# The Mamba-2 scan of one diffusion trunk step on one core: masks made by TensorE, ln dt in the exponents, outputs three steps behind

## Chip, cores and metric

One NeuronCore of a Trainium2 chip runs the whole kernel as one launch. The metric is the device time of a launch in microseconds (us); smaller is better.

## The reference, cut to what matters

The kernel computes four layers of a diffusion backbone for 128 context tokens and 256 latent tokens. Layer 1 mixes its tokens with a bidirectional Mamba-2 scan (SSD), and the change touches that layer alone. For each direction the scan is, in chunks of 128 tokens:

```python
acs = jnp.cumsum(dtc * a.reshape(SSD_GROUPS, r), axis=2)
seg = acs[:, :, :, None] - acs[:, :, None, :]
decay = jnp.exp(jnp.where(lower, seg, -jnp.inf))
cb = jnp.einsum('bcign,bcjgn->bcijg', cc, bc)
wts = cb[..., None] * decay * dtc[:, :, None]
y_diag = jnp.einsum('bcijgr,bcjgrp->bcigrp', wts, xc)
to_end = jnp.exp(acs[:, :, -1:] - acs) * dtc
chunk_states = jnp.einsum('bcjgn,bcjgr,bcjgrp->bcgrpn', bc, to_end, xc)
y_off = jnp.einsum('bcign,bcgrpn->bcigrp', cc, h_prev) * jnp.exp(acs)[..., None]
```

There are 32 heads of 64 in 8 groups of 4 heads, a state of 128, and two directions (forward f, backward b), whose outputs are added. The result is multiplied by silu(z), normalised and multiplied by `ssd_w_out`.

## The kernel before, in words

The program is written by hand, engine by engine, and counting semaphores order the work. Matrices of the layers are float32 split into a high and a low float32r part: ScalarE (ACT) rounds each chunk of weights of 128 x 1024 (`round_to`, L829), and POOL and VectorE (DVE) subtract one half each (`low_to`, L700 and L1183). TensorE (PE) makes three products per tile. Four chunks are held at once.

The SSD layer has these stages. `ssd_conv` makes x, B and C. `dt_prepare` makes 16 z tiles (PE, about 4.25 us each), and beside them dt, the running sums of dt times a (`neg_cum`, `back_cum`), and at its end the tables `to_end` and `full_decay` (ACT L959, L960, DVE L1381). The scan then runs 24 steps: for each of 8 groups g, chunk c = 0 (the context), 1 and 2 (the two latent halves); u = 3g + c counts steps and v counts latent steps. In each step u the engines do, in program order:

- PE (`scan_pe`): three transposes and C times B into bank u % 2 (L1854 to L1857); the chunk state of step u - 1 (L1842, two products when c = 0, else one); for each direction four products that spread the running sum of one head over a 128 x 128 square (L1866, stationary adt, moving the triangle tri, float32) into bank 2 + d; and the output of step u - 2 (L1833). An output has per head two terms of `x_dt` times `decay`, and for a latent chunk two more of a state times `c_scaled`: 16 products of 64 stationary columns in a latent step, 8 in a context step.
- ACT (`scan_act`): copies bank u % 2 to SBUF (L969); for latent chunks two exponentials of 512 columns (L975) for `c_scaled`; four Relu of 128 columns for the backward exponents (L981); two exponentials of 512 columns (L990).
- DVE (`scan_dve`): `take_state(u - 1)` (L1407, or L1415 and L1420); two triangular masks of C times B (L1430); four forward exponents of 128 columns (L1439); after each exponential a product with the masked C times B (L1449); the output of step u - 2 into xbc (L1394).
- POOL (`scan_pool`): `x_end` (L740, two when c = 0), `x_dt` of both directions (L748), and for latent chunks two products of `c_scaled` with C (L756).
- SP (`scan_traffic`) loads a group's start state and stores its context state, 256 KB each; its queue also carries all weight loads.

`ssd_end` then runs over 16 tiles m of y: DVE multiplies by silu(z) (L1469) and makes `y_lo` of tile m - 1 (L1464); ACT squares (L998) and rounds (`y_hi`, L999); POOL adds the squares (L766, L769). In each m every engine also prepares weight chunk m + 2 of `ssd_out`:

```python
for m in range(KI):
    low_to(n0 + min(m + 3, KI))
    pool.wait_ge(y_sq_ready, m + 1)
```

PE makes `ssd_out` beside this (L1727 to L1729, 18 products of 512 columns per chunk, 288 in all), waits for each `y_lo` and weight chunk, and before chunk 12 for the sum of squares (L1892).

Of the kernel before, what the change touches and what calls it, by code (L numbers as in the profile page):

```python
# [14 lines left out]
P = 128  # L15
# [27 lines left out]
SCAN_LAG = 2  # L43
SCAN_SLOTS = SCAN_LAG + 1
DT_DVE = 20
# [33 lines left out]
SLOTS = 4  # L79
# [67 lines left out]
def build_trunk(nc, a, out):  # L147
# [4 lines left out]
    with ExitStack() as ctx:  # L152
# [7 lines left out]
        h_hi = sb("h_hi", [P, KD, COLS], F32R)  # L160
        h_lo = sb("h_lo", [P, KD, COLS], F32R)
# [7 lines left out]
        rowc = sb("rowc", [P, D])  # L169
        junk = sb("junk", [P, D], BF16)  # L170
# [47 lines left out]
        with ExitStack() as part:  # L218
            zt = sb("zt", [P, KI, COLS], F32, part)
            xbc = sb("xbc", [P, CONV_TILES, COLS], F32, part)  # L220
            state0 = sb("state0", [P, 2, 2, GW], F32, part)
            dtv = sb("dtv", [P, 3, NDT], F32, part)
            adt = sb("adt", [P, 3, NDT], F32, part)
            neg_cum = sb("neg_cum", [P, 3, NDT], F32, part)
            back_cum = sb("back_cum", [P, 3, SSD_HEADS], F32, part)
# [42 lines left out]
        decay = [by_dir(flat_mod[:, k * 1024:(k + 1) * 1024]) for k in range(SCAN_SLOTS)]  # L268
        c_scaled = [by_dir(flat_mod[:, 3072:4096]), by_dir(flat_gb[:, 1024:2048])]
        turned = flat_gb[:, 0:1024].rearrange("p (u n) -> p u n", u=2)  # L270
        x_dt = [by_dir(flat_wk[:, k * 512:(k + 1) * 512]) for k in range(SCAN_SLOTS)]
# [4 lines left out]
        state1 = by_dir(flat_stage[:, 896:1408])  # L276
        cb_mask = by_dir(flat_stage[:, 1408:1664])
# [82 lines left out]
        s_seg_back = sem("s_seg_back")  # L360
        s_exp = sem("s_exp")
        s_w = sem("s_w")
        s_xdt = sem("s_xdt")
# [107 lines left out]
        def z_bank(m):  # L471
            return bank((2, 3, 7)[m % 3])

# [218 lines left out]
        def _(pool):  # L692
# [39 lines left out]
            def scan_pool():  # L732
                for g, c, u, v in steps():
                    pool.wait_ge(s_copied, u + 1)
                    xt = turned[:, u % 2, P:P + GW].rearrange("p (h q) -> p h q", h=HPG)
# [8 lines left out]
                    if u >= SCAN_SLOTS:  # L744
                        pool.wait_ge(s_y, u - SCAN_SLOTS + 1)
                    for d in range(2):
                        h0 = d * SSD_HEADS + g * HPG
                        pool.tensor_tensor(x_dt[u % SCAN_SLOTS][:, d, :].rearrange("p (h q) -> p h q", h=HPG), xt,  # L748
                                           dtv[:, c, h0:h0 + HPG].unsqueeze(2).broadcast_to([P, HPG, HEAD]),
                                           ALU.mult).then_inc(s_xdt, 1)  # L750
                    if c:
                        for d in range(2):
                            pool.wait_ge(s_cexp, 2 * v + d + 1)
                            cs = c_scaled[v % 2][:, d, :].rearrange("p (h i) -> p h i", h=HPG)
# [64 lines left out]
        def _(act):  # L819
# [128 lines left out]
            def dt_prepare():  # L948
# [9 lines left out]
                act.wait_ge(z_dt, DT_DVE - 1)  # L958
                act.activation(to_end, to_end, ACT.Exp).then_inc(dt_act, 1)  # L959
                act.activation(full_decay, full_decay, ACT.Exp).then_inc(dt_act, 1)  # L960

            def scan_act():
                for g, c, u, v in steps():
                    act.wait_ge(s_turned, u + 1)
                    if u >= 2:
                        act.wait_ge(s_state, u - 1)
                        act.wait_ge(s_xdt, 2 * (u - 1))
                        act.wait_ge(s_w, 2 * (u - 2) + 2)
                    act.activation(turned[:, u % 2, :], bank(u % 2), ACT.Copy).then_inc(s_copied, 1)  # L969
                    if c:  # L970
                        if v >= 2:
                            act.wait_ge(s_y, latent_step(v - 2) + 1)
                        for d in range(2):
                            act.wait_ge(s_cum, 2 * u + d + 1)
                            act.activation(c_scaled[v % 2][:, d, :], bank(2 + d), ACT.Exp).then_inc(s_cexp, 1)  # L975
                    if u >= SCAN_SLOTS:
                        act.wait_ge(s_y, u - SCAN_SLOTS + 1)
                    act.wait_ge(s_cum, 2 * u + 2)
                    for h in range(HPG):
                        hs = slice(h * P, (h + 1) * P)  # L980
                        ins = act.activation(decay[u % SCAN_SLOTS][:, 1, hs], bank(3)[:, hs], ACT.Relu, scale=-1.0,  # L981
                                             bias=back_cum[:, c, g * HPG + h:g * HPG + h + 1])
                    ins.then_inc(s_seg_back, 1)
                    for d in range(2):
                        if d:
                            act.wait_ge(s_seg_back, u + 1)
                        else:
                            act.wait_ge(s_seg, u + 1)
                        w = decay[u % SCAN_SLOTS][:, d, :]
                        act.activation(w, w, ACT.Exp, scale=-1.0 if d else 1.0).then_inc(s_exp, 1)  # L990

            def ssd_end():
                n0 = lin["ssd_out"].n0
                for m in range(KI):
# [6 lines left out]
                    round_to(n0 + min(m + 3, KI))  # L1001
# [169 lines left out]
        def _(vec):  # L1171
# [168 lines left out]
            def dt_prepare():  # L1340
# [26 lines left out]
                link(vec.scalar_tensor_tensor(out=adt[:, :, :], in0=rowc[:, 960:1024].unsqueeze(1).broadcast_to([P, 3, NDT]),  # L1367
                                              scalar=-1.0, in1=dtv[:, :, :], op0=ALU.mult, op1=ALU.mult))
                assert n[0] == DT_DVE - 2
# [867 lines left out]
```

## Time and profile before

| what | value |
|---|---|
| time, median of 3 runs | 2129.44 us (2127.71 to 2131.0) |
| time of the profiled execution | 2127.83 us |
| its span | 2126.1 us |
| PE busy | 1967.0 us, 93% |
| DVE / ACT / POOL busy | 58% / 44% / 35% |
| granted PE clock, mean | 0.965 |
| the scan, first to last PE or DVE instruction | 637.3 to 783.4 us |
| `ssd_out` on PE | 785.9 to 875.9 us |

The span is what the trace covers; the time has 1.7 us more around it. An engine's busy time counts its own instructions alone. Times in the views are in us from the start of the span; "xN" is a count of records, and a float32 product of PE leaves two records, a float32r product one. The length of a PE record holds its way through the array; the distance between the starts of two records is what the stream pays.

### The profile page before, as it was taken

The numbers are of one execution on the slowest core, as the hardware profiler recorded it, in microseconds if no ns is written. First come the engines' busy times: TensorE is split into PE (matmuls) and PEld (weight loads), VectorE is DVE, ScalarE is ACT, GpSimd is POOL, SyncE is SP. The second block draws the span as 40 slices with busy tenths as digits, with TensorE's granted clock in tenths as the row PEclk, the third lists the DMA queues.
The fourth block names the chain that finished last, engine by engine and source line by source line (L and its number), as shares of the span: only waits on it lengthen the run. The fifth ranks groups of instructions, "written<-read, shape, count | busy, mean of one in ns | idle before, by whom it ended". The sixth has DMA issues, their size and how long they took to land.

```text
span 2126.1 us, 30500 instructions
## 1 busy us (share of the span) xinstructions
PE 1967.0 (93%) x11921; PEld 1752.3 (82%) x11921; DVE 1237.2 (58%) x1888; ACT 926.9 (44%) x1522; POOL 736.8 (35%) x563
## 2 busy tenths in 40 slices
PE   3779999999998878899999998899999979899998
PEld 1569998799997876699988875699987857799986
DVE  0567771466617867677742873777733675677732
ACT  1244442444536644454432534544433434544422
POOL 0033334332346646232333651233233321233242
PEclk6889999999999999999999999999999979999999
DMA  9963437544330123743455564543454512244432
GB/s 367 385 234 122 128 101 247 178 129 123 107 113 26 31 114 120 280 147 120 128 184 192 201 193 157 222 148 120 129 201 159 207 55 100 80 141 127 121 127 79
DMA packets 80671, 326.44 MB, mean 154 GB/s; under 512 B 9073, under 2 KB 17809, under 8 KB 66705
## 3 DMA queue, kind: packets, MB, share of 16 engines
q1 hardware_dynamic: 78928, 322.57, 43.7%
q8 instruction: 95, 1.56, 0.3%
q10 hardware_dynamic: 1600, 1.93, 0.3%
q14 instruction: 48, 0.39, 0.1%
HBM read 319.34 MB, written 5.12 MB: 153 GB/s over the span
## 4 chain that ended last, share of the span: by engine, by line
PE 78%; DVE 7%; ACT 5%; DMA 4%; issue 4%; POOL 3%; SPq 1%; DVEq 0%; ACTq 0%; POOLq 0%
PE pair L1693 17%; PE pair L1695 17%; PE pair L1694 17%; PE pair L1728 6%; PE pair L1727 6%; PE pair L1729 6%; PE pair L1833 2%; DVE x L1250 1%; DMA mod_more<-in_w_mod 1%; PE pair L1915 1%; POOL w_lo L700 1%; PE pair L1866 1%; DMA raw<-in_pool 1%; ACT junk L857 1%; DMA ssd_cols<-in_ssd_cols 1%
## 5 line engine op out<-in xcount | busy, mean ns | idle before, releaser
L700 POOL TENSOR_TENSOR w_lo<-raw,w_hi 128x512 fp32r<-128x512 f32 (+1 forms) x375 | 575.5, 1536 | 1165.3 <-ACT w_hi L829 1165.3
L1693 PE MATMUL pair<-h_hi,w_hi 128*128 128x386 f32 (+1 forms) x2008 | 689.0, 343 | 18.3 <-POOL h_lo L707 15.7
L1695 PE MATMUL pair<-h_hi,w_lo 128*128 128x386 f32 (+1 forms) x2008 | 684.6, 341 | 0.0
L1694 PE MATMUL pair<-h_lo,w_hi 128*128 128x386 f32 (+1 forms) x2008 | 683.9, 341 | 0.0
L1183 DVE TENSOR_TENSOR w_lo<-raw,w_hi 128x512 fp32r<-128x512 f32 x351 | 427.4, 1220 | 331.7 <-ACT w_hi L829 331.6
L829 ACT ACTIVATE w_hi<-raw 128x1024 fp32r<-128x1024 f32 x375 | 393.1, 1050 | 285.9 <-PE pair L1729 222.7
L1693 PEld LDWEIGHTS pair<-h_hi,w_hi 128*128 128x128 f32 (+1 forms) x2008 | 381.7, 190 | 23.7 <-POOL h_lo L707 21.6
L1694 PEld LDWEIGHTS pair<-h_lo,w_hi 128*128 128x128 f32 (+1 forms) x2008 | 382.3, 190 | 0.9
L1695 PEld LDWEIGHTS pair<-h_hi,w_lo 128*128 128x128 f32 (+1 forms) x2008 | 381.6, 190 | 0.3
L1307 DVE SCALAR_TENSOR_TENSOR acc<-pair,taps,acc 128x385 f32<-128x385 f32 x176 | 109.0, 619 | 214.1 <-ACT acc L916 214.1
L916 ACT ACTIVATE acc<-pair,taps 128x386 f32<-128x386 f32 x176 | 117.2, 666 | 237.9 <-PE pair L1695 237.9
L1728 PE MATMUL pair<-w_hi,g 128*128 128x512 f32 x528 | 208.6, 395 | 0.0
L1729 PE MATMUL pair<-w_lo,g 128*128 128x512 f32 x528 | 208.6, 395 | 0.0
L1727 PE MATMUL pair<-w_hi,g 128*128 128x512 f32 x528 | 208.5, 395 | 0.0
L1728 PEld LDWEIGHTS pair<-w_hi,g 128*128 128x128 f32 x528 | 99.4, 188 | 23.2
L1727 PEld LDWEIGHTS pair<-w_hi,g 128*128 128x128 f32 x528 | 99.3, 188 | 23.3
L1729 PEld LDWEIGHTS pair<-w_lo,g 128*128 128x128 f32 x528 | 99.3, 188 | 23.2
L914 ACT ACTIVATE g<-gate 128x386 fp32r<-128x386 f32 x84 | 44.3, 528 | 162.4 <-DVE gate L1320 162.4
L1314 DVE SCALAR_TENSOR_TENSOR acc<-pair,taps,acc 128x385 f32<-128x385 f32 x176 | 108.6, 617 | 3.2
L707 POOL TENSOR_TENSOR h_lo<-stage,h_hi 128x512 fp32r<-128x512 f32 x21 | 32.0, 1522 | 88.9 <-ACT h_hi L879 88.9
L1833 PE MATMUL pair<-mod_raw,wk 128*64 128x128 f32 x384 | 45.4, 293 | 16.2 <-DVE stage L1420 9.7
L1664 PE MATMUL pair<-mod_raw,cond 128*32 128x256 f32 x512 | 36.4, 425 | 23.3 <-DMA mod_raw<-in_w_mod 23.3
(251 smaller groups left out, 2302.2 us busy)
## 6 DMA issues: line engine op xcount, KB each, us to landing
raw<-in_ffn_in SPq DMA_DIRECT2D x176, 512.0 KB, 3.5
raw<-in_ffn_out SPq DMA_DIRECT2D x88, 512.0 KB, 3.5
mod_raw<-in_w_mod SPq DMA_DIRECT2D x32, 1024.0 KB, 7.7
mod_base<-in_w_mod SPq DMA_DIRECT2D x31, 1024.0 KB, 7.4
mod_more<-in_w_mod SPq DMA_DIRECT2D x20, 1024.0 KB, 13.0
raw<-in_ssd_conv SPq DMA_DIRECT2D x32, 512.0 KB, 3.5
gb<-rows_dram SPq DMA_DIRECT2D x8, 1024.0 KB, 5.0
raw<-in_ssd_z SPq DMA_DIRECT2D x16, 512.0 KB, 3.5
```

The source lines that it names most:

```text
L700: pool.tensor_tensor(w_lo[:, m % SLOTS, 0:w], raw[:, m % SLOTS, 0:w], w_hi[:, m % SLOTS, 0:w].bitcast(F32), ALU.subtract).then_inc(w_low_p ...
L829: act.activation(w_hi[:, m % SLOTS, 0:w], raw[:, m % SLOTS, 0:w], ACT.Copy).then_inc(w_rounded, 1)
L916: act.activation(acc[:, j % 4, :], tile_bank(j)[:, 0:COLS], ACT.Identity, scale=taps[:, l, j, 1:2], bias=taps[:, l, j, 3:4]).then_inc(acc_ ...
L1183: vec.tensor_tensor(w_lo[:, m % SLOTS, w0:w1], raw[:, m % SLOTS, w0:w1], w_hi[:, m % SLOTS, w0:w1].bitcast(F32), ALU.subtract).then_inc(w_ ...
L1307: vec.scalar_tensor_tensor(out=acc[:, j % 4, 1:COLS], in0=b[:, 0:COLS - 1], scalar=taps[:, l, j, 0:1], in1=acc[:, j % 4, 1:COLS], op0=ALU. ...
L1314: vec.scalar_tensor_tensor(out=acc[:, j % 4, 0:COLS - 1], in0=b[:, 1:COLS], scalar=taps[:, l, j, 2:3], in1=acc[:, j % 4, 0:COLS - 1], op0= ...
L1693: ten.matmul(to, wh, h_hi[:, k, cols], start=k == 0, stop=False, skip_group_check=True)
L1694: ten.matmul(to, wh, h_lo[:, k, cols], start=False, stop=False, skip_group_check=True)
L1695: ins = ten.matmul(to, wl, h_hi[:, k, cols], start=False, stop=k == KD - 1, skip_group_check=True)
L1727: ten.matmul(to, hi[:, k, cols], wh, start=first, stop=False)
L1728: ten.matmul(to, lo[:, k, cols], wh, start=False, stop=False)
L1729: ins = ten.matmul(to, hi[:, k, cols], wl, start=False, stop=last)
```

## The change

- The running sums are made once as rows (`cum_rows`, a float32r high part and a low part in other partitions; 12 float32 products into bank 4 in `dt_prepare`), and PE spreads a head's row with the 0/1 column of `head_row` (float32r, 128 columns moving). A further float32r product of 512 moving columns (`outside_of`) adds -2^100 outside the triangle, after ACT has read the bank for `c_scaled` where c > 0.
- The exponents get `shift` = ln dt minus the running sum as ACT's bias, so x needs no product with dt, and ACT writes both directions with 8 exponentials of 128 columns (`one_way`). DVE adds the two directions and multiplies the sum once with C times B, which it reads from PSUM. A head's output has one term for both directions in place of two.
- DVE in place of ACT copies bank u % 2 (384 columns of it), at the head of its step.
- The exponents go round banks 2, 3 and 7; PE waits for `s_exp` (ACT). Outputs are three steps behind and come in two halves between the `outside_of` products. `turned` and `decay` have 4 slots, `c_scaled` 3, `state1` 2.
- Ln of dt, the exponentials of `to_end` and `full_decay` and the copy of `cum_rows` are in ACT's order after z tiles 3 and 6.
- `ssd_end` prepares a weight chunk at m = 8, 10, 12 and 14 and the rest after the loop.

The diff, cut (leading blanks taken off):

```diff
-SCAN_LAG = 2
+SCAN_LAG = 3
 SCAN_SLOTS = SCAN_LAG + 1
-DT_DVE = 20
+C_SLOTS = 3
+DT_ADT = 18
+DT_DVE = DT_ADT + 3
+FAR = 2.0 ** 100
+DT_LEAST = 1e-37
...
-neg_cum = sb("neg_cum", [P, 3, NDT], F32, part)
-back_cum = sb("back_cum", [P, 3, SSD_HEADS], F32, part)
+shift = sb("shift", [P, 3, NDT], F32, part)
+ident_r = sb("ident_r", [P, P], F32R, part)
+outside = sb("outside", [P, 2, P], F32R, part)
...
+decay = [flat_mod[:, k * 512:(k + 1) * 512] for k in range(SCAN_SLOTS)]
+one_way = [[flat_mod[:, 2048 + d * 1024 + k * 512:2560 + d * 1024 + k * 512] for d in range(2)] for k in range(2)]
...
+state1 = [[under_h_lo[:, 2 * k + d, AT[1]:AT[1] + GW] for d in range(2)] for k in range(2)]
...
+def seg_bank(u, d):
+
+return bank((2, 3, 7)[(2 * u + d) % 3])
...
-        if u >= SCAN_SLOTS:
-            pool.wait_ge(s_y, u - SCAN_SLOTS + 1)
-        for d in range(2):
-            h0 = d * SSD_HEADS + g * HPG
-            pool.tensor_tensor(x_dt[u % SCAN_SLOTS][:, d, :].rearrange("p (h q) -> p h q", h=HPG), xt,
-                               dtv[:, c, h0:h0 + HPG].unsqueeze(2).broadcast_to([P, HPG, HEAD]),
-                               ALU.mult).then_inc(s_xdt, 1)
...
-        low_to(n0 + min(m + 3, KI))
+        low_to(n0 + SLOTS + max(0, m - 6) // 2)
...
+    low_to(n0 + KI)
...
         z_evac(m)
-    act.wait_ge(z_dt, DT_DVE - 1)
-    act.activation(to_end, to_end, ACT.Exp).then_inc(dt_act, 1)
-    act.activation(full_decay, full_decay, ACT.Exp).then_inc(dt_act, 1)
+        if m == 3:
+            act.wait_ge(z_dt, DT_ADT + 1)
+            act.activation(log_dt, log_dt, ACT.Ln).then_inc(dt_act, 1)
+        if m == 6:
+            act.wait_ge(z_dt, DT_DVE - 1)
+            act.activation(to_end, to_end, ACT.Exp).then_inc(dt_act, 1)
+            act.activation(full_decay, full_decay, ACT.Exp).then_inc(dt_act, 1)
+            act.wait_ge(dt_pe, 3)
+            act.activation(cum_rows[:, :, :], bank(4)[:, 0:3 * P].rearrange("p (c i) -> p c i", c=3),
+                           ACT.Copy).then_inc(dt_act, 1)
...
     for g, c, u, v in steps():
-        act.wait_ge(s_turned, u + 1)
...
-        act.activation(turned[:, u % 2, :], bank(u % 2), ACT.Copy).then_inc(s_copied, 1)
...
-        act.wait_ge(s_cum, 2 * u + 2)
...
-            ins = act.activation(decay[u % SCAN_SLOTS][:, 1, hs], bank(3)[:, hs], ACT.Relu, scale=-1.0,
-                                 bias=back_cum[:, c, g * HPG + h:g * HPG + h + 1])
-        ins.then_inc(s_seg_back, 1)
+                act.activation(c_scaled[v % C_SLOTS][:, d, :], seg_bank(u, d), ACT.Exp).then_inc(s_cexp, 1)
         for d in range(2):
-            if d:
-                act.wait_ge(s_seg_back, u + 1)
-            else:
-                act.wait_ge(s_seg, u + 1)
-            w = decay[u % SCAN_SLOTS][:, d, :]
-            act.activation(w, w, ACT.Exp, scale=-1.0 if d else 1.0).then_inc(s_exp, 1)
+            act.wait_ge(s_seg, 2 * u + d + 1)
+            if u >= 2:
+                act.wait_ge(s_sum, u - 1)
+            to = one_way[u % 2][d]
+            for h in range(HPG):
+                hs = slice(h * P, (h + 1) * P)
+                col = d * SSD_HEADS + g * HPG + h
+                ins = act.activation(to[:, hs], seg_bank(u, d)[:, hs], ACT.Exp, bias=shift[:, c, col:col + 1])
+            ins.then_inc(s_exp, 1)
...
+    link(vec.tensor_scalar(log_dt, flat_dt, DT_LEAST, None, ALU.max))
...
+    ch.did(vec.tensor_tensor(head_row[:, :].rearrange("p (d h) -> p d h", d=2), halves[:, :, 0, :],
...
+    ch.did(vec.tensor_copy(ident_r[:, :], ident[:, :]))
+    ch.did(vec.tensor_scalar(outside[:, :, :], tri[:, :, :], 1.0, FAR, ALU.subtract, ALU.mult))
...
-    ch.did(vec.tensor_scalar(neg_cum[:, :, :], cum, -1.0, None, ALU.mult))
+    vec.wait_ge(dt_act, 3)
     ch.did(vec.tensor_copy(full_decay, total))
-    ch.did(vec.tensor_copy(back_cum[:, :, :], cum[:, :, SSD_HEADS:]))
+    ch.did(vec.scalar_tensor_tensor(out=shift[:, :, :], in0=cum, scalar=-1.0,
+                                    in1=log_dt.rearrange("p (c h) -> p c h", c=3), op0=ALU.mult, op1=ALU.add))
     ch.wait()
-    link(vec.tensor_tensor(to_end, full_decay, neg_cum[:, :, :], ALU.add))
+    link(vec.tensor_tensor(to_end, full_decay, cum, ALU.subtract))
+    low_to(lin["ssd_z"].n0 + 10)
+    vec.wait_ge(dt_act, 6)
+    link(vec.tensor_tensor(to_end, to_end, dtv[:, :, :], ALU.mult))
+    for d in range(2):
+        low_rows = slice((2 * d + 1) * SSD_HEADS, (2 * d + 2) * SSD_HEADS)
+        vec.tensor_tensor(cum_rows[low_rows, :, :], bank(4)[low_rows, 0:3 * P].rearrange("p (c i) -> p c i", c=3),
+                          cum_rows[low_rows, :, :].bitcast(F32), ALU.subtract).then_inc(s_rows, 1)
     low_to(lin["ssd_out"].n0 + SLOTS)
-    vec.wait_ge(dt_act, 4)
-    link(vec.tensor_tensor(to_end, to_end, dtv[:, :, :], ALU.mult))
...
-        if g:
-            vec.wait_ge(s_y, 3 * g)
+        if g >= 2:
...
+        vec.wait_ge(s_turned, u + 1)
...
+        vec.tensor_copy(turned[u % SCAN_SLOTS][:, 0:P + GW], bank(u % 2)[:, 0:P + GW]).then_inc(s_copied, 1)
...
-        vec.wait_ge(s_copied, u + 1)
-        if u:
-            vec.wait_ge(s_w, 2 * u)
-        for d in range(2):
-            ch.did(vec.tensor_tensor(cb_mask[:, d, :], turned[:, u % 2, P + GW:], tri[:, d, :], ALU.mult))
-        masks = ch.n
-        if u >= SCAN_SLOTS:
-            vec.wait_ge(s_y, u - SCAN_SLOTS + 1)
...
-        for h in range(HPG):
-            col = g * HPG + h
-            ins = vec.tensor_scalar(decay[u % SCAN_SLOTS][:, 0, h * P:(h + 1) * P], bank(2)[:, h * P:(h + 1) * P],
-                                    neg_cum[:, c, col:col + 1], 0.0, ALU.add, ALU.min)
...
-        for d in range(2):
-            vec.wait_ge(s_exp, 2 * u + d + 1)
-            w = decay[u % SCAN_SLOTS][:, d, :].rearrange("p (h i) -> p h i", h=HPG)
-            vec.tensor_tensor(w, w, cb_mask[:, d, :].unsqueeze(1).broadcast_to([P, HPG, P]),
-                              ALU.mult).then_inc(s_w, 1)
+        vec.wait_ge(s_exp, 2 * u + 2)
+        to = decay[u % SCAN_SLOTS]
+        vec.tensor_tensor(to, one_way[u % 2][0], one_way[u % 2][1], ALU.add).then_inc(s_sum, 1)
+        vec.wait_ge(s_sum, u + 1)
+        w = to.rearrange("p (h i) -> p h i", h=HPG)
+        vec.tensor_tensor(w, w, bank(u % 2)[:, P + GW:].unsqueeze(1).broadcast_to([P, HPG, P]),
+                          ALU.mult).then_inc(s_w, 1)
         if u >= SCAN_LAG:
             output(*ALL_STEPS[u - SCAN_LAG][:3])
...
+    for c in range(3):
+        for d in range(2):
+            hs = slice(d * SSD_HEADS, (d + 1) * SSD_HEADS)
+            for rows in range(2 * d, 2 * d + 2):
+                ins = ten.matmul(bank(4)[rows * SSD_HEADS:(rows + 1) * SSD_HEADS, c * P:(c + 1) * P],
+                                 adt[:, c, hs], tri[:, d, :], start=True, stop=True, skip_group_check=True)
+    ins.then_inc(dt_pe, 1)
...
+    def output(g, c, u, v, heads):
+        if heads[0] == 0:
...
+            ten.wait_ge(s_w, u + 1)
...
+        for h in heads:
...
-            terms = [(x_dt[u % SCAN_SLOTS][:, d, hs], decay[u % SCAN_SLOTS][:, d, ws]) for d in range(2)]
+            terms = [(turned[u % SCAN_SLOTS][:, P + h * HEAD:P + (h + 1) * HEAD], decay[u % SCAN_SLOTS][:, ws])]
             if c:
...
+        if heads[-1] == HPG - 1:
+            ins.then_inc(s_y, 1)
+
+    def outside_of(u, d):
+        ten.matmul(seg_bank(u, d), ident_r[:, :], outside[:, d, :].unsqueeze(1).broadcast_to([P, HPG, P]),
+                   start=False, stop=True, skip_group_check=True).then_inc(s_seg, 1)
...
+            ten.wait_ge(s_w, u - 1)
...
         if u:
             states((u - 1) % 3, u - 1)
         for d in range(2):
-            if u:
-                ten.wait_ge((s_seg, s_seg_back)[d], u)
+            i = 2 * u + d - 3
+            if i >= 0:
+                ten.wait_ge(s_exp, i + 1)
             for h in range(HPG):
                 col = d * SSD_HEADS + g * HPG + h
-                ins = ten.matmul(bank(2 + d)[:, h * P:(h + 1) * P],
-                                 adt[:, c, col:col + 1].broadcast_to([P, P]), tri[:, d, :],
-                                 start=True, stop=True, skip_group_check=True)
+                ins = ten.matmul(seg_bank(u, d)[:, h * P:(h + 1) * P], head_row[:, col:col + 1].broadcast_to([P, P]),
+                                 cum_rows[:, c, :], start=h == 0, stop=False, skip_group_check=True)
             ins.then_inc(s_cum, 1)
-        if u >= SCAN_LAG:
-            output(*ALL_STEPS[u - SCAN_LAG])
+            if not c:
+                outside_of(u, d)
+        for d in range(2):
+            if u >= SCAN_LAG:
+                output(*ALL_STEPS[u - SCAN_LAG], range(2 * d, 2 * d + 2))
+            if c:
+                ten.wait_ge(s_cexp, 2 * v + d + 1)
+                outside_of(u, d)
     states(2, 3 * GROUPS - 1)
     for step in ALL_STEPS[-SCAN_LAG:]:
-        output(*step)
+        output(*step, range(HPG))
```

## Rows read from the trace of the kernel before

**Rows 1.** By stretch of the scan: PE, PEld, DVE, ACT, POOL busy; clock; DMA.

```profile
637.28:650.49 13.21, 11.64 (x85) 10.68 (x86) 8.55 (x20) 8.45 (x21) 7.97 (x11) 0.87 0.06 20
650.49:775.75 125.26, 108.10 (x1061) 99.55 (x1060) 103.22 (x258) 76.04 (x180) 84.30 (x102) 0.99 0.09 29
775.75:783.42 7.67, 7.02 (x64) 6.78 (x64) 1.21 (x4) 0.00 (x0) 0.00 (x0) 0.65 0.01 2
```

**Rows 2.** Chain of waits in the scan: start us, us, what.

```profile
707.88 2.54 PE pair L1833 x32
...
723.88 0.43 DVE stage L1420
...
742.03 2.54 PE pair L1833 x32
```

**Rows 3.** Timeline of steps: start us, us, engine, line [idle before, releaser].

```profile
699.77 1.95 PE L1866 MATMUL pair<-tri,adt 128*128 128x128 f32 x16
...
700.92 0.60 ACT L975 ACTIVATE gb<-pair 128x512 f32<-128x512 f32 x1 [0.79 <-PE pair L1866]
...
702.25 1.14 ACT L981 ACTIVATE mod_raw<-pair,back_cum 128x128 f32<-128x128 f32 x4
...
702.72 0.33 PE L1854 MATMUL pair<-ident,xbc 128*128 128x128 f32 x1
...
703.33 0.60 PE L1842 MATMUL pair<-wk,gb 128*128 128x256 f32 x2
...
709.52 1.15 ACT L990 ACTIVATE mod_raw<-mod_raw 128x512 f32<-128x512 f32 x2 [2.57 <-DVE mod_raw L1439]
...
710.25 1.29 DVE L1449 TENSOR_TENSOR mod_raw<-mod_raw,stage 128x512 f32<-128x512 f32 x2 [0.77 <-ACT mod_raw L990]
...
711.46 0.60 DVE L1394 SCALAR_TENSOR_TENSOR xbc<-xbc,ssd_cols,pair 128x128 f32<-128x128 f32 x2
...
712.02 0.69 DVE L1407 COPY stage<-pair 128x512 f32<-128x512 f32 x1
...
739.31 1.64 POOL L740 TENSOR_TENSOR wk<-gb,stage 128x256 f32<-128x256 f32 x2 [0.41 <-ACT gb L969]
```

**Rows 4.** Timeline of the last z tile's end and of the scan's first instruction.

```profile
633.38 0.49 ACT L945 ACTIVATE zt<-pair 128x386 f32<-128x386 f32 x1 [2.81 <-PE pair L1695]
...
637.28 0.30 PE L1854 MATMUL pair<-ident,xbc 128*128 128x128 f32 x1 [3.94 <-DVE stage L1381]
```

**Rows 5.** Timeline of float32r products in a row, of 512 and 256 moving columns.

```profile
811.49 0.40 PE L1728 MATMUL pair<-w_hi,y_lo 128*128 128x512 f32 x1
...
811.72 0.40 PE L1729 MATMUL pair<-w_lo,y_hi 128*128 128x512 f32 x1
...
1723.44 0.28 PE L1996 MATMUL pair<-w_hi,h_lo 128*128 128x256 f32 x1
1723.56 0.28 PE L1997 MATMUL pair<-w_lo,h_hi 128*128 128x256 f32 x1
```

**Rows 6.** DVE lines of the scan: ns min/median/max, first and last start.

```profile
L1449 DVE TENSOR_TENSOR mod_raw<-mod_raw,stage x48: 677/692/1124, 643.2 to 773.5; 128x512 f32<-128x512 f32 x48
...
L1420 DVE TENSOR_TENSOR stage<-stage,pair x16: 420/421/423, 650.3 to 775.1; 128x256 f32<-128x256 f32 x16
```

**Rows 7.** Timeline of ssd_out, its two long waits.

```profile
799.18 0.77 PE L1727 MATMUL pair<-w_hi,y_hi 128*128 128x512 f32 x1 [4.73 <-DVE y_lo L1464]
...
855.38 0.77 PE L1892 MATMUL pair<-ones,stage 128*128 128x1 f32 x3 [7.61 <-POOL stage L769]
```

**Rows 8.** Lines of ssd_end and ssd_out: ns min/median/max, first and last start.

```profile
L1469 DVE TENSOR_TENSOR xbc<-xbc,zt x16: 553/1647/1657, 783.4 to 852.4; 128x386 f32<-128x386 f32 x16
...
L1729 PE MATMUL pair<-w_lo,y_hi x96: 386/394/629, 786.5 to 875.5; 128*128 128x512 f32 x96
```

**Rows 9.** Groups by line, 783 to 856 us: busy, mean ns, idle before.

```profile
L700 POOL TENSOR_TENSOR w_lo<-raw,w_hi 128x512 fp32r<-128x512 f32 x12 | 21.5, 1792 | 29.0 <-ACT w_hi L829 29.0
...
L829 ACT ACTIVATE w_hi<-raw 128x1024 fp32r<-128x1024 f32 x12 | 12.6, 1050 | 12.8 <-DMA raw<-in_ssd_out 7.2 <-PE pair L1729 5.6
```

More of the change, by code:

```diff
@@ L160, in build_trunk @@
         h_hi = sb("h_hi", [P, KD, COLS], F32R)
+        with ExitStack() as part:
+            under_h_lo = sb("under_h_lo", [P, KD, COLS], F32, part)
         h_lo = sb("h_lo", [P, KD, COLS], F32R)
@@ L169, in build_trunk @@
         rowc = sb("rowc", [P, D])
+        with ExitStack() as part:
+            cum_rows = sb("cum_rows", [P, 3, P], F32R, part)
+            head_row = sb("head_row", [P, NDT], F32R, part)
         junk = sb("junk", [P, D], BF16)
@@ L266, in by_dir @@
             return ap.rearrange("p (d n) -> p d n", d=2)
[L268 to L271, printed above, removed]
+        decay = [flat_mod[:, k * 512:(k + 1) * 512] for k in range(SCAN_SLOTS)]
+        one_way = [[flat_mod[:, 2048 + d * 1024 + k * 512:2560 + d * 1024 + k * 512] for d in range(2)] for k in range(2)]
+        c_scaled = [by_dir(flat_gb[:, 1024:2048]), by_dir(flat_wk[:, 512:1536]), by_dir(rowc[:, :])]
+        turned = [flat_gb[:, 0:512], flat_gb[:, 512:1024], flat_wk[:, 0:512], flat_stage[:, 1408:1920]]
+        adt = flat_wk[:, 512:704].rearrange("p (c h) -> p c h", c=3)
+        log_dt = flat_wk[:, 704:896]
         x_end = by_dir(flat_wk[:, 1536:2048])
@@ L1432, in scan_dve @@
-                    if u >= SCAN_SLOTS:
-                        vec.wait_ge(s_y, u - SCAN_SLOTS + 1)
-                    vec.wait_ge(s_cum, 2 * u + 1)
-                    if c:
-                        vec.wait_ge(s_cexp, 2 * v + 1)
-                    for h in range(HPG):
-                        col = g * HPG + h
-                        ins = vec.tensor_scalar(decay[u % SCAN_SLOTS][:, 0, h * P:(h + 1) * P], bank(2)[:, h * P:(h + 1) * P],
-                                                neg_cum[:, c, col:col + 1], 0.0, ALU.add, ALU.min)
-                        if h == HPG - 1:
-                            ins.then_inc(s_seg, 1)
-                        else:
-                            ch.did(ins)
@@ L1828, in output @@
                         if c:
                             for d in range(2):
-                                st = state0[:, g % 2, d, hs] if d == c - 1 else state1[:, d, hs]
-                                terms.append((st, c_scaled[v % 2][:, d, ws]))
+                                st = state0[:, g % 2, d, hs] if d == c - 1 else state1[g % 2][d][:, hs]
+                                terms.append((st, c_scaled[v % C_SLOTS][:, d, ws]))
                         for n, (lhs, rhs) in enumerate(terms):
@@ L1841, in states @@
                     for d in state_dirs(c):
-                        ins = ten.matmul(bank(6)[:, d * GW:(d + 1) * GW], turned[:, u % 2, 0:P], x_end[:, d, :],
+                        ins = ten.matmul(bank(6)[:, d * GW:(d + 1) * GW], turned[u % SCAN_SLOTS][:, 0:P], x_end[:, d, :],
                                          start=True, stop=True, skip_group_check=True)
@@ L1898, in free @@
                     ten.wait_ge(s_taken, 3 * GROUPS)
-                    ten.wait_ge(s_exp, 6 * GROUPS)
+                    ten.wait_ge(s_w, 3 * GROUPS)
                 out_product(sums, 2, y_hi, y_lo, ready, free)
```

66 lines of the change are left out of this document (29 added, 37 removed).

## The prediction, made before the changed kernel was built

> **What bounds the kernel now.** I read the busy times by stretch first. The scan lasts 146.1 us [rows 1]: 13.2 for three steps without an output, 125.3 in the middle, 7.7 at the end. In the middle PE is busy 86% and DVE 82%, so neither engine alone sets the pace. The chain of waits says what does: it repeats every 34.15 us for six steps (742.03 - 707.88), 17.08 us per group [rows 2], and goes from PE's outputs through ACT's Relu and exponentials to DVE's products and `take_state` and back to PE. In each step DVE works before the exponentials (masks, forward exponents) and after them, and PE waits for its last piece. The second stretch is `ssd_out`: 18 products a chunk at 0.23 us [rows 5] are 4.19 us, 67 us in all, but it lasts from 785.9 to 875.9 [rows 8], 90 us. PE waits 4.7 us for a `y_lo` and 7.6 us for the sum of squares [rows 7], some 0.7 us at each of four more tiles, and after each long wait runs slower: the products there take 0.77 us, not 0.40 [rows 5, 7]. The cause is that each tile of y stands in line behind a weight chunk on three engines.
>
> **The scan, engine by engine.** Prices per product of PE are distances of starts: transposes with C times B 0.61, a state product 0.44, four spread products 0.89, which is 0.222 each (1.95 us record groups less the last record's length, 16 records at 0.111) [rows 3]. A latent output of 16 products takes 2.54 us [rows 2].
>
> The spread products turn from float32 to float32r with 128 moving columns, which no row shows. From below: 256 columns cost 0.12 and 512 cost 0.23 [rows 5], a line that gives 0.062 at 128. From above: the old price, 0.222; nothing but that row caps it. I take 0.11, the distance of two weight loads of 128 columns within a float32 product, since such a load is now needed every 128 columns. The Trainium skill's page "TensorE: Matmul & The Clock Gate", section on LDWEIGHTS, makes a load of 128 columns 107 ns; by it the sum stays as it is, by the line of the moving columns alone it falls by 6 us.
>
> PE after, per step: eight spread products 0.89; two masks of 512 columns 0.46 [rows 5]; a latent output of 12 products, 12/16 of 2.54, 1.9, plus 0.2 for two more changes between 64 and 128 stationary columns (estimate), so outputs with masks 2.6; a context output 0.64. A context step is 0.61 + 0.44 + 0.89 + 0.46 + 0.64 = 3.04, the first latent 0.61 + 0.88 + 0.89 + 2.6 = 4.98, the second 4.54: 12.6 us per group. ACT: eight exponentials of 128 columns, 2.3 a step, as four Relu cost 1.14 [rows 3], plus 1.2 in latent steps: 9.3. DVE: copy 0.55 (384 of the 512 columns that cost 0.69), add and multiply 1.3, output 0.6, state 0.8: 9.8 a group, where it was 14.1 (82% of 17.08). POOL loses its two `x_dt` products per step. All three would fit beside PE.
>
> **The chain after.** What is late next is DVE's queue. The copy of step u + 1 stands behind the add and multiply of step u, which wait for ACT's last exponential, and that for PE's second mask. From PE's second mask of a second latent step: to ACT 0.26 (eight records from 699.77, ACT at 700.92), exponentials 1.14, to DVE 0.1, add and multiply 1.3, output 0.56, copy 0.55, to POOL 0.1, two `x_end` 1.64, to PE 0.2 [rows 3]: 5.85. DVE's add reads two operands from SBUF. The old product that does so takes 0.68 to 1.12 us, while a line with one operand in PSUM never leaves 0.42 [rows 6]; the long ones lie beside POOL's. POOL then holds a `c_scaled` product, 1.1 long, so I add 0.9 (bounds 0 and 1.2): 6.75. The Trainium skill's page "SBUF — State Buffer", section "SBUF: two separate sides", says that such an op and a GpSimd op exclude each other for a whole instruction. By this rule, which speaks against the new add, the period stays at my figure; without it it is 0.9 shorter. The rows agree.
>
> PE can take the context state only then, though its own work reaches that point after 3.65. Then: state 0.88, spread 0.89, output with masks 2.6 = 4.37, and the next latent step 4.54, whose states come in time. The group takes 6.75 + 4.37 + 4.54 = 15.7, against 17.1. The other new waits are covered: transposes wait for `s_w` of two steps before (2.8 after the mask, with the hop at 3.05, when PE is ready for them), the third bank's `s_exp` lies over 1 us back, the masks' wait for `s_cexp` lies beside half an output. SP's load of a start state waits for an output that comes one step later, but is used three steps on, some 15 us; the store of a context state has as long.
>
> Whole scan: three steps to fill, 13.2 scaled by 15.7/17.1, 12.1; seven groups 109.9. The end: DVE reaches the last `take_state` 4.3 after the last mask, 0.8 more, 0.25 to PE; the last two outputs, 32 products in 7.0 us at clock 0.65 [rows 1], are 24 now, 5.3 (0.65 is a mean of the clock's two levels, 1.2 and 2.4 GHz, after PE's wait, and I leave it so); DVE 0.8: 11.4. Sum 133.4, so **-12.7**.
>
> **Start.** PE sat 3.94 us at the scan's start for DVE L1381, after ACT's table and exponentials [rows 4]. These move under the z tiles, where ACT is idle 2.81 us per tile [rows 4] and its four table loads and the new waits on DVE and PE fit in; DVE's and POOL's next weight halves come about 1 us later but lie four chunks ahead, and SP's loads are freed by them with the same lead. If that cover failed it would cost up to 3 us. PE then starts after the last z evacuation, 633.9, so 3.3 earlier. The 12 new products are on PE's path: between 0.7 (four column groups side by side) and 2.7 (12 x 0.222), I take 1.0. **-2.3**.
>
> **ssd_out.** Without a chunk a tile costs DVE 0.55 and 0.6 (its minimum [rows 8]) and POOL 0.9, and these exclude each other: 2.0. Tile 8 comes at 799.5; its product, squares and rounding 1.7, round 1.05, low half 1.8 [rows 9]: chunk 4 is there at 804.0, PE wants it at 785.9 + 4 x 4.19 = 802.7: wait 1.3. From there two tiles and one chunk take 2.0 + 0.55 + 1.1 + 1.05 + 1.8 = 6.5 against 4.19: 2.3 for each of three chunks; then 0.3. Waits 8.5, products 67, unit transposes and sums 1.6: 77, not 90. In the rows no slow products follow the waits of 0.7 us; for waits of 2 us no row speaks, I count nothing and leave 3 us in the bounds. I take **-12.5** (bounds: -17 if nothing waits, -5 if tiles take 2.7 or the clock falls). `y_lo` and the sum are early, so 5 MB of loads for the next stage also start early; I count nothing for it.
>
> **Sum.** -12.7 - 2.3 - 12.5 = -27.5. The profiled execution is 2127.8 (span 2126.1 + 1.7), so 2100.3; the median is 1.6 above it, so **2102**.
>
> **Rivals.**
> - *Narrow float32r at the full old price* (0.222). For: no row below 256 columns. Against: 256 and 512 lie on a line. 16 products of the latent steps gain 0.11 less, 1.8 per group, 14 us in all: 2116. Chance 0.15.
> - *The DVE queue does not bind*, since copies come earlier than I think: PE's 12.6 per group, 3.1 x 7.8 = 24 less: 2078. For: DVE is 60% busy. Chance 0.25.
> - *The weights only change places*: tiles stay slow, PE waits for chunks 4 to 7 instead of `y_lo`, gain 5: 2110. This is the case where the change does not do what it says. Chance 0.10.
> - *Slower*: a float32r product with 128 moving columns that costs more than the float32 one it replaces. It stands in PE's order before the masks, on the chain above, 16 times a group, about 125 times. It decides from 0.11 + 27.5/125 = 0.33 us; at 0.40 the time is 2138. Against: the rows' line. Chance 0.04.
> - The rest, 0.46, is my forecast, of which 0.02 for gains lost to causes I don't see.
>
> **Numbers.** The range 2074 to 2118 reaches from below the PE-bound case (with the 0.062 price 2072 is possible) to above the dear float32r, and leaves out the slower case and the far ends. About 0.2% is what a measurement here tells from no change. Faster by more than that 0.94, within it 0.02, slower 0.04.
>
> **What would show it.** Scan near 133 us; a group near 15.7; spread products 0.11 apart; PE waiting for POOL's `x_end` before the context state, and nowhere else for long; PE's first scan instruction at most 0.6 after the last z evacuation; `ssd_out` near 77 us with waits for weights at chunks 4 to 7 and none for the sum of squares. The forecast is wrong if the spread products stand 0.2 apart, if PE waits for DVE's output or `take_state` in each step, or if z tiles grow beyond 4.25 us.

## The result, and the profile after the change

The changed kernel takes **2118.31 us** (median of 5 runs, 2116.47 to 2122.18); the kernel before, in 5 runs, 2129.93 (2127.71 to 2131.0). The ratio is 0.9949, 95% interval 0.9935 to 0.9964: 11.6 us faster, where 27.5 were forecast, and 0.3 us outside the range given. The profiled execution took 2119.51 us (span 2117.8); its mean granted clock is 0.954, where it was 0.965.

The busy times by stretch of the new scan, in the columns of [rows 1]: up to the first output, the middle, from the last state on. As outputs now lag by three steps, the first stretch holds four steps, where it held three.

```profile
636.90:654.20 17.30, 15.08 (x68) 12.55 (x68) 9.88 (x17) 11.62 (x33) 8.88 (x10) 0.70 0.04 16
654.20:778.95 124.75, 111.03 (x748) 91.15 (x748) 63.86 (x134) 61.36 (x191) 51.40 (x55) 0.82 0.09 29
778.95:790.50 11.55, 7.02 (x59) 6.08 (x58) 5.07 (x13) 1.14 (x4) 2.20 (x2) 0.70 0.00 0
```

Against [rows 1], DVE is busy 51% of the middle, not 82%, and PE 89%, although it has fewer products. The column of the clock says why: 0.82, where it was 0.99. The scan lasts 153.6 us, not 146.1 and not the forecast 133.4. One group in the timeline (start, length, engine, line; idle time before and releaser in brackets):

```profile
705.26 1.39 DVE L1449 TENSOR_TENSOR mod_raw<-mod_raw 128x512 f32<-128x512 f32 x1 [1.65 <-ACT mod_raw L993]
...
707.81 0.55 DVE L1444 COPY gb<-pair 128x384 f32<-128x384 f32 x1
...
708.44 1.78 POOL L754 TENSOR_TENSOR wk<-gb,stage 128x256 f32<-128x256 f32 x2 [2.33 <-DVE gb L1444]
...
710.32 1.10 PE L1859 MATMUL pair<-wk,gb 128*128 128x256 f32 x4 [2.06 <-POOL wk L754]
...
711.07 1.77 PE L1885 MATMUL pair<-cum_rows,head_row 128*128 128x128 f32 x8
...
714.73 0.80 PE L1850 MATMUL pair<-outside,ident_r 128*128 128x512 f32 x1
...
718.00 0.42 PE L1872 MATMUL pair<-ident,xbc 128*128 128x128 f32 x1
```

The forecast chain is there: add (L1449), copy behind it, POOL's `x_end`, then PE's context state, 6.5 us after the last mask of the second latent step (started at 703.55, its 512 columns 0.23 us, so about 703.8). But PE has stood idle for 2.06 us, and the latent step that follows takes 7.7 us, 710.32 to 718.00: its mask is a record of 0.80 us, where one of the step before took 0.50. The granted clock by stretch of the same group: the context step, the wait, the first latent step, the second.

```profile
704.00:707.50 3.50, 2.98 (x26) 2.40 (x25) 2.20 (x3) 2.90 (x11) 2.11 (x2) 1.00 0.47 150
707.50:710.30 2.80, 0.74 (x5) 0.58 (x6) 2.73 (x7) 0.42 (x2) 1.78 (x2) 1.00 0.00 0
710.30:718.00 7.70, 7.68 (x38) 6.21 (x39) 1.84 (x5) 2.34 (x6) 2.76 (x3) 0.58 0.02 4
718.00:722.80 4.80, 4.80 (x42) 4.08 (x41) 3.12 (x7) 3.33 (x10) 0.90 (x2) 0.97 0.00 0
```

A granted clock of 0.58 over the step means that most of it runs at the lower of the clock's two levels, 1.2 GHz; in the next step, at 0.97, 2.4 GHz is back. The waits of PE from the end of the z tiles to the end of `ssd_out` (in total, times, longest):

```profile
PE pair L1859 <- POOL wk L754: 14.5, 7, 2.2
PE pair L1845 <- DVE under_h_lo L1437: 3.8, 1, 3.8
PE pair L1731 <- POOL w_lo L714: 3.4, 2, 2.3
PE pair L1731 <- DVE y_lo L1467: 3.2, 1, 3.2
```

The start of the scan, against [rows 4], and `ssd_out`, against [rows 7, 8]:

```profile
636.35 0.49 ACT L953 ACTIVATE zt<-pair 128x386 f32<-128x386 f32 x1 [2.81 <-PE pair L1699]
...
636.90 0.33 PE L1872 MATMUL pair<-ident,xbc 128*128 128x128 f32 x1 [0.58 <-ACT zt L953]
...
821.03 0.50 PE L1731 MATMUL pair<-w_hi,y_hi 128*128 128x512 f32 x1 [1.15 <-POOL w_lo L714]
...
827.77 0.80 PE L1731 MATMUL pair<-w_hi,y_hi 128*128 128x512 f32 x1 [2.29 <-POOL w_lo L714]
...
850.32 0.72 PE L1916 MATMUL pair<-ones,stage 128*128 128x1 f32 x6
```

```profile
L1472 DVE TENSOR_TENSOR xbc<-xbc,zt x16: 545/1228/1654, 790.5 to 826.5; 128x386 f32<-128x386 f32 x16
...
L1733 PE MATMUL pair<-w_lo,y_hi x96: 387/394/632, 793.6 to 868.4; 128*128 128x512 f32 x96
```

PE has been idle for 0.58 us when it begins, and nearly all of that is the last z evacuation itself: it ends at 636.84, and PE begins at 636.90. The tiles of y come in 36 us, not 69; the sum of squares keeps nobody waiting; two waits for weights are left. The span's 8.3 us, by stretch (each z evacuation taken by its start): before the z evacuations +2.0 (nothing in the change touches that part; over the profiled executions of all kernels here the last z evacuation starts anywhere from 633.4 to 640.1), z tiles 65.1 to 66.1, +1.0; to PE's first scan instruction 3.9 to 0.55, -3.35; the scan +7.5; from there to the end of `ssd_out` 92.5 to 78.3, -14.2; the rest -1.2.

### The profile page after: what moved, and what is told of

The parts are those of the page before. It is cut to its first block, busy times and chain, and to the rows that moved or that the text cites. A ratio compares the mean times of both kernels' runs of the same rounds, so it can differ in the third digit from the quotient of the medians.

```text
span 2117.8 us, 29692 instructions
## 1 busy us (share of the span) xinstructions
PE 1975.0 (93%) x11609; PEld 1745.0 (82%) x11609; DVE 1199.7 (57%) x1773; ACT 920.3 (43%) x1552; POOL 703.9 (33%) x515
## 4 chain that ended last, share of the span: by engine, by line
PE 81%; DVE 6%; ACT 4%; DMA 3%; issue 3%; POOL 2%; SPq 1%; DVEq 0%; ACTq 0%; POOLq 0%
PE pair L1697 17%; PE pair L1699 17%; PE pair L1698 17%; PE pair L1731 6%; PE pair L1732 6%; PE pair L1733 6%; PE pair L1845 2%; DVE x L1255 2%; DMA mod_more<-in_w_mod 1%; PE pair L1939 1%; ACT junk L865 1%; DMA raw<-in_pool 1%; PE pair L1885 1%; PE pair L1850 1%; DVE wk L1246 1%
## 5 line engine op out<-in xcount | busy, mean ns | idle before, releaser
L993 ACT ACTIVATE mod_raw<-pair,shift 128x128 f32<-128x128 f32 x192 | 53.8, 375 | 33.4 <-PE pair L1850 33.2
```

## The experiments

Three questions: does the wait cost its length, or also the clock behind it; what makes the wait; and are the other two parts worth what was forecast? Each measured time stands against a median of the kernel before from the same chip; kernels compared with the same median ran on one chip. An idle product is one whose result nothing reads.

### The other two parts alone

`e4_end_only` is the kernel before with only the new places of the weight halves:

```diff
-                    low_to(n0 + min(m + 3, KI))
+                    low_to(n0 + SLOTS + max(0, m - 6) // 2)
...
+                low_to(n0 + KI)
```

(on DVE and POOL, and the same with `round_to` on ACT).

> The kernel before with only the last part of the change, the place of the weight chunks' halves among the tiles of y in ssd_out. Theory: this part alone gives 12 to 14 us whatever the scan does: ssd_out from 90 us to 76 to 78, kernel 2116 to 2118, so that the new scan and the new start are together worth nothing. Rival (it gains only because the changed scan leaves other conditions, banks and DVE free earlier): less than 6 us, 2124 or more.

Measured 2117.29 us against 2130.48, ratio 0.9938 (0.9924 to 0.9951): -13.2. The part does not need the new scan.

`e8_start_only` is the kernel before with only this (and, on DVE, the product behind it, with the weight halves placed round it as in the changed kernel):

```diff
                 for m in range(1, KI):
                     z_evac(m)
-                act.wait_ge(z_dt, DT_DVE - 1)
-                act.activation(to_end, to_end, ACT.Exp).then_inc(dt_act, 1)
-                act.activation(full_decay, full_decay, ACT.Exp).then_inc(dt_act, 1)
+                    if m == 6:
+                        act.wait_ge(z_dt, DT_DVE - 1)
+                        act.activation(to_end, to_end, ACT.Exp).then_inc(dt_act, 1)
+                        act.activation(full_decay, full_decay, ACT.Exp).then_inc(dt_act, 1)
```

> The kernel before with only ACT's table and exponentials for the decays (and DVE's product behind them) moved under the z tiles; no new rows, no new products. Theory: PE starts the scan 0.6 us after the last z evacuation instead of 3.9, so 3.3 us are gained if nothing later takes them back: 2127 us. Rival (the first steps of the scan wait for DVE anyway): no change, 2130.

Measured 2126.68 against 2130.27, ratio 0.9982 (0.9973 to 0.9991): -3.6. With the 1.0 us of the small products these two parts make -15.8, more than the whole change's 11.6. So the new scan did not pay: it takes 7.5 us longer in the profiled execution. In the medians it costs some 4 us, a sum of three differences whose 95% intervals (about 3, 3 and 2 us to either side) together leave it uncertain by nearly 5, if the parts add up at all.

### The wait filled, and nothing else

`e5_fill` adds to the changed kernel, on PE:

```diff
+                def fillers(b, n):
+                    for _ in range(n):
+                        ten.matmul(b[:, 0:2 * P], ident_r[:, :], cum_rows[:, 0:2, :], start=True, stop=True,
+                                   skip_group_check=True)
...
+                    if c == 1:
+                        if u > 1:
+                            ten.wait_ge(s_exp, 2 * u - 2)
+                        fillers(seg_bank(u, 0), 16)
                     if u:
                         states((u - 1) % 3, u - 1)
```

> The changed kernel, its order untouched, with 16 idle float32r products of 256 columns (about 1.9 us by 0.12 each) on PE in the one long wait of each group, between the transposes and the context state, into a bank that ACT has done with. Nothing of the computation changes. Theory (the clock): that wait of 2.06 us lets the clock fall, and the first latent step then takes 7.7 us instead of 4.4; filled, the step is back at 4.4, the group at about 15.7 instead of 19.0, the kernel at 2118 - 7 x 3.3 = 2095 us, granted clock in the scan near 1. Rival A (the products of that step are slow in themselves): nothing moves, 2118. Rival B (DVE and POOL set the period, the clock costs nothing on the path): the step shrinks but the waits grow by as much, 2118.

Measured 2101.73 against 2130.12, ratio 0.9863 (0.9847 to 0.988): 16.6 us below the changed kernel, for work that computes nothing. A group of it in the timeline:

```profile
702.47 2.15 PE L1851 MATMUL pair<-cum_rows,ident_r 128*128 128x256 f32 x16
704.77 1.10 PE L1864 MATMUL pair<-wk,gb 128*128 128x256 f32 x4 [0.15 <-issue]
705.52 1.19 PE L1894 MATMUL pair<-cum_rows,head_row 128*128 128x128 f32 x8
...
709.57 0.27 PE L1877 MATMUL pair<-ident,xbc 128*128 128x128 f32 x1
```

The state comes as long after the mask as in the changed kernel (6.5 us), but the step behind it takes 4.8 us, not 7.7. Rivals A and B both fall: the same products are fast, and the time comes off the period. With the clock held, the scan, 639.4 to 773.2, takes **133.8 us**; the forecast was 133.4. `e10_fill_four` has 4 such products instead of 16.

> The changed kernel with 4 idle products (0.5 us) in each group's wait, not 16, so that 1.6 us of it stay. If a wait of 1.6 us is as bad as one of 2.06: 2118, groups of 19.0 us with half speed after the wait. If the shorter wait leaves the clock alone: 2101, as with 16. I lean to something between, since in e7_wait_back one and the same wait of 2.33 us let the clock fall in some groups and not in others: 2110.

Measured 2105.21 against 2130.27, ratio 0.9876 (0.9858 to 0.9893), with one execution at 2097.6. Waits of 1.58 us are left. From context state to context state the profiled execution takes 15.7 to 16.1 us three times, 17.1 and 17.6, and 19.2 once. In this execution the shorter wait brought the slow stretch less often.

### What makes the wait

`e2_copy_first` moves one instruction of DVE in the changed kernel: step u + 1's copy goes ahead of the add and multiply of step u.

```diff
+                copy(0)
                 for g, c, u, v in steps():
-                    vec.wait_ge(s_turned, u + 1)
-                    if u >= SCAN_SLOTS:
-                        vec.wait_ge(s_y, u - SCAN_SLOTS + 1)
-                    vec.tensor_copy(turned[u % SCAN_SLOTS][:, 0:P + GW], bank(u % 2)[:, 0:P + GW]).then_inc(s_copied, 1)
                     if u:
                         take_state(*ALL_STEPS[u - 1][:3])
+                    if u + 1 < 3 * GROUPS:
+                        copy(u + 1)
                     vec.wait_ge(s_exp, 2 * u + 2)
```

(`copy(u)` is the four lines taken out.)

> The changed kernel with DVE's copy of step u + 1 ahead of the add and multiply of step u. Theory (the copy behind the add and multiply is what delays POOL's x_end and so the context state): POOL is free of c_scaled some 2.3 us after the second mask, x_end 1.7, so the state can start about 4.2 us after the mask instead of 6.5; PE then waits only some 0.6 us for the multiply before its transposes. With the clock at full the group is 3.6 + 0.6 + 4.4 + 4.5 = 13.2 us, the kernel 2118 - 8 x 5.8 = 2072. If the clock falls all the same, only the 2.1 us of the wait go: 2101. Rival (POOL, not DVE's order, is late): 2112 to 2118.

`e3_act_copy` leaves DVE's order and gives the copy back to ACT, ahead of the step's exponentials:

```diff
+                    act.wait_ge(s_turned, u + 1)
+                    if u >= SCAN_SLOTS:
+                        act.wait_ge(s_y, u - SCAN_SLOTS + 1)
+                    act.activation(turned[u % SCAN_SLOTS][:, 0:P + GW], bank(u % 2)[:, 0:P + GW], ACT.Copy).then_inc(s_copied, 1)
                     if c:
```

> The changed kernel with the copy of the turned operands back on ACT, ahead of its exponentials of the step, as before the change. Theory: the copy of the context step is then 1.4 + 0.5 us after the second mask, x_end done at about 4.1, group 13.2 to 13.6 us, kernel 2072 to 2078, with the clock at full. ACT carries some 11 us of work per group. Rival (ACT becomes the bound, since its copy of a latent step stands behind the exponentials and the masks wait for them): group 16 or more, 2095 or more. Rival (the queue of DVE does not matter): 2118.

Measured 2084.17 (ratio 0.9787, 0.9773 to 0.98) and 2083.4 (0.9786, 0.9767 to 0.9805), against 2130.48. Taking the copy out from behind the add, either way, gives 34 us over the changed kernel. In `e2_copy_first`:

```profile
706.27 0.56 DVE L1444 COPY stage<-pair 128x384 f32<-128x384 f32 x1 [1.25 <-PE pair L1880]
...
706.89 0.69 DVE L1454 TENSOR_TENSOR mod_raw<-mod_raw 128x512 f32<-128x512 f32 x1
...
706.91 1.72 POOL L754 TENSOR_TENSOR wk<-stage 128x256 f32<-128x256 f32 x2 [1.40 <-DVE stage L1444]
...
709.76 1.10 PE L1864 MATMUL pair<-wk,stage 128*128 128x256 f32 x4 [0.46 <-DVE under_h_lo L1437]
```

The copy now comes before the add, POOL is done at 708.6, and PE's wait is 0.46 us, for `take_state`. Five groups, from context state to context state, of the changed kernel, of `e5_fill` and of `e2_copy_first`, in that order:

```profile
671.44:767.84 96.40, 85.31 (x546) 69.90 (x546) 47.53 (x101) 45.17 (x140) 38.29 (x40) 0.79 0.09 28
```

```profile
673.03:752.18 79.15, 76.79 (x625) 65.10 (x626) 48.40 (x101) 44.52 (x140) 38.28 (x40) 1.00 0.11 35
```

```profile
668.15:737.48 69.33, 67.08 (x546) 55.66 (x546) 48.02 (x101) 44.61 (x140) 41.08 (x40) 1.00 0.13 39
```

That is 19.3, 15.8 and 13.9 us a group. The 546 records of PE are the same in the first and the third; only the clock is 0.79 or 1.00, and they are busy 85.3 or 67.1 us. The estimate of 2072 was 12 us too low: 13.9 instead of 13.2 a group is 5 of them; the rest is its count of eight groups at the full gain, while the first group and the scan's ends gain little.

### The wait put back

`e7_wait_back` has in the fast kernel four idle POOL products ahead of each context step's `x_end`:

```diff
+                    for k in range(4 if u and not c else 0):
+                        pool.tensor_tensor(under_h_lo[:, 4 + k, AT[1]:AT[1] + GW].rearrange("p (h q) -> p h q", h=HPG), xt,
+                                           to_end[:, c, g * HPG:(g + 1) * HPG].unsqueeze(2).broadcast_to([P, HPG, HEAD]),
+                                           ALU.mult)
```

> The kernel with the copy first (e2_copy_first) with four more POOL products of 256 columns ahead of each context step's x_end (their results are not used), so that PE's wait before the context state is about 2.3 us again, 1.9 more than the 0.46 it is there. Theory (the clock): the wait costs 1.9 and the slow step after it 3.3 per group, 5.2 x 7 = 36 us: 2120 us, with a granted clock near 0.8 in the scan. Rival (a wait costs its own length and no more): 1.9 x 7 = 13 us, 2097.

Measured 2112.38 against 2130.12, ratio 0.9923 (0.9902 to 0.9943): 28 us above `e2_copy_first`, nearer to the theory's 36 than to 13. The trace shows the rest:

```profile
692.16 1.10 PE L1868 MATMUL pair<-wk,gb 128*128 128x256 f32 x4 [2.33 <-POOL wk L758]
...
707.91 2.04 PE L1868 MATMUL pair<-wk,gb 128*128 128x256 f32 x4 [2.34 <-POOL wk L758]
```

```profile
702.00:707.90 5.90, 3.58 (x30) 2.89 (x29) 5.19 (x10) 3.30 (x12) 4.78 (x7) 1.00 0.28 89
707.90:716.00 8.10, 8.09 (x40) 6.61 (x41) 1.38 (x4) 2.33 (x6) 2.75 (x3) 0.58 0.01 3
```

One wait of 2.33 us leaves the state's record at 1.10 us, and the next context state comes 15.75 us later; after the next wait, of 2.34 us, it is 2.04, at a clock of 0.58, and the group takes 18.87 us. The other groups took 18.87, 17.23 and 17.25. A wait of one length comes with the slow stretch or without. The two parts can be told apart here: 15.75 is the 13.9 of `e2_copy_first` and the 1.88 us by which the wait grew, all of it at the full clock; the 3.1 us more of the groups of 18.87 are the clock's.

### The ends of the scan

`e6_fill_start` is `e2_copy_first` with 17 idle products in the wait of 2.16 us of the first context state alone; `e9_combined` has besides that the last `take_state` ahead of the last add and multiply, 8 idle products before the last two outputs and 24 after them:

```diff
+                    if u == 1:
...
+                        fillers(seg_bank(u, 0), 17)
...
                 states(2, 3 * GROUPS - 1)
+                output(*ALL_STEPS[-SCAN_LAG], range(HPG))
+                ten.wait_ge(s_exp, 6 * GROUPS - 1)
+                fillers(seg_bank(3 * GROUPS, 0), 8)
-                for step in ALL_STEPS[-SCAN_LAG:]:
+                for step in ALL_STEPS[1 - SCAN_LAG:]:
                     output(*step, range(HPG))
+                fillers(seg_bank(3 * GROUPS, 0), 24)
...
+                    if u == 3 * GROUPS - 1:
+                        take_state(*ALL_STEPS[-1][:3])
                     vec.wait_ge(s_exp, 2 * u + 2)
...
-                take_state(*ALL_STEPS[-1][:3])
```

> The kernel with the copy first (e2_copy_first, 2084 us) with 17 idle products in the wait of 2.16 us of the first context state alone. Theory (the clock): the records of the next 11 us, which are at half speed there, go back to full: some 5 us less, 2079. Rival (PE waits for ACT and DVE in the fill of the pipeline anyway): 2083 to 2084.

> The kernel with the copy first, the filled first wait, the last take_state ahead of the last add and multiply on DVE, 8 idle products before the last two outputs and 24 after them. Theory: 5 us from the start, 2.7 us less wait and 1.4 us less slow clock at the tail, 1.5 us less slow clock at the head of ssd_out: 2084 - 10 = 2074. Rival (what the scan's ends give is taken back by ssd_out, whose first tiles do not come earlier): 2079.

Measured 2087.79 and 2083.77 against 2130.12 (0.98, 0.9786 to 0.9815; 0.9783, 0.9768 to 0.9798). Both lie above what the theory and its rival gave, and `e6_fill_start` is no faster than `e2_copy_first`. So `e2_copy_first` and `e9_combined` ran once more, side by side.

> The same kernel as e2_copy_first, beside the next one on the same chip. 2084 to 2086 us.

> The same kernel as e9_combined. From the last z evacuation to the first tile of y it took 116.2 us in e9_combined and 121.5 in e2_copy_first, so it should be 5 us faster than e11_copy_again here; if the two are within 2 us, the gain of the scan's two ends is given back behind the scan.

Measured 2084.62 (0.9782, 0.9768 to 0.9795) and 2084.37 (0.9784, 0.977 to 0.9797) against 2130.27. In the traces the stretch from the last z evacuation to the first tile of y does shrink, 122.3 to 116.2 us here, and `ssd_out` takes 78 and 77 us behind it; the two profiled executions are 5.2 us apart (2088.32 and 2083.13), yet the medians are equal. The profiled execution of `e11_copy_again` was the slowest of its five, which spread over 7 us, and that of `e12_combined_again` the fastest of its four. By the medians the ends are worth little or nothing; where the 5 us of the traces go in the other executions stays open.

## Why the prediction was wrong, by its own steps

**The step that failed** is the 4.37 us of the first latent step, "state 0.88, spread 0.89, output with masks 2.6": prices from rows at the full clock, put behind a wait of PE that the same sum had made. The scan had no term for the clock ahead of its tail. The remark on waits of 2 us stood under `ssd_out` only, with 3 us in the bounds. The step measured 7.7 us in the group shown. At the full clock, in `e5_fill`, it takes 4.80, so 0.4 of the miss is the price of the products and 2.9 the clock. The five groups average 19.3 us, 3.6 above the forecast 15.7. With the wait filled the group is 15.8 and the scan 133.8 us. That one term is worth 20 us of the scan, 16.6 in the medians; without it the forecast of 2102 would have stood beside 2101.73. That the two are so near is in part luck: as the next paragraphs show, errors inside the group and inside `ssd_out` cover each other.

**Why it looked safe**: the kernel before has waits of 2.16 us in its scan too, in every other group, and a clock of 1.00 behind the one shown:

```profile
707.88 0.62 PE L1833 MATMUL pair<-mod_raw,wk 128*64 128x128 f32 x4 [2.16 <-POOL wk L748]
```

```profile
705.70:707.88 2.18, 0.02 (x2) 0.04 (x1) 2.15 (x7) 1.14 (x4) 2.18 (x4) 1.00 0.01 4
707.88:712.00 4.12, 4.12 (x43) 3.85 (x44) 3.35 (x9) 1.75 (x3) 0.42 (x1) 1.00 0.02 4
```

There PE had just streamed the step's eight spread products in float32, 16 records [rows 3]; in the changed kernel it comes from a context step with eight in float32r, at half the price, and in the group shown from a wait of 0.55 us just before. That this is the reason is not shown: PE had waits of 2.06 us with slow steps in groups where no such short wait is listed, and in `e7_wait_back` a wait of 2.33 us behind the same products went both ways. The Trainium skill's page "TensorE: Matmul & The Clock Gate", section on the HAM clock gate, says that the gate follows how busy PE has lately been. The runs agree in that idle products alone brought the full clock back. I had cited that page for weight loads and not for this. So a row that shows a wait without a slow stretch is no price for a wait as long in another place.

**Right in the scan**: the chain (forecast 6.75 us from mask to context state, measured 6.5; 6.2 and 6.5 by turns in `e5_fill`) and what is late in it, the copy behind the add; PE waiting for `x_end` once a group, and after the fill nowhere else over 0.6 us until the tail. The add beside a POOL product took 1.39 us, not 0.69: 0.7 more, where I had 0.9; in the other groups it was 0.1 to 0.7 more. The second latent step took 4.8 (4.54). At the full clock the chain was thus 0.2 to 0.6 us shorter than forecast and the two latent steps together 0.6 longer, and the group of 15.8 is near the forecast 15.7 because these cover each other. Eight spread products took 1.19 us as a group of records, which is 0.11 apart once the last record, 0.27, is taken off: the narrow float32r rival falls, and so does the slower one.

**The rival that DVE's queue does not bind** (2078) is what `e2_copy_first` builds: 2084. In the changed kernel the queue binds, through one copy's place. I had the mechanism, and gave the case 0.25 for a wrong reason, that copies might come earlier of themselves.

**Start**: forecast -2.3; by the trace -3.35 and +1.0. **ssd_out**: forecast 77 us from its first product to its last, where it was 90, and -12.5; measured 75.8 (792.98 to 868.8), 78.3 from the end of the scan, so -14.2, and -13.2 alone. The size is in part luck again. Its waits for weights were 1.15 and 2.29, 3.4 us and not the forecast 8.5; but the products ran at the lower clock at the start of `ssd_out` and behind the longer wait (records of 0.5 to 0.8 us, not 0.39), which took some 3 us that the sum did not have (17 distances of starts, most of them 0.43 and not 0.23). That is inside the bound I had left. The rival that the weights only change places falls.

## What to carry to other kernels

When a sum gives PE a new wait, or less work around an old one, price the step behind it at both levels of the clock from rows of either, and carry the slow one as a rival with a chance of its own. Making each engine's work smaller isn't enough where an in-order queue decides: ask of each instruction that frees another engine whether it stands behind one that waits. To tell a wait from the clock behind it, fill the wait with products that nobody reads.

## What the runs showed of the hardware

- The length of a wait does not decide by itself whether the clock falls behind it: 2.33 us did and did not in neighbouring groups of one execution; 2.16 did not in the kernel before; 2.06 did, for part of a step or for most of it, in the changed one; of five waits of 1.58 us two were followed by groups of 15.7 us, two by 17.1 and 17.6, one by 19.2. What tips it was not settled.
- Idle products of 2.15 us gave back 3.5 us a group (19.3 to 15.8).
- An add of two SBUF operands of 128x512 on DVE took 0.68 to 1.42 us in the changed kernel, the longest beside a POOL product that was already running; with the copy on ACT it took 0.69 in all 24 steps, and POOL was idle when each began. The delay can fall on the other engine: at 709.07 an add began as POOL's first `x_end` product ended and took 0.68, and the second `x_end` product took 1.09 us, where the first had taken 0.73.
